# Leaving out TensorE's idle products in a two-layer mixer and expert trunk

## The reference

```python
for layer in range(DEPTH):
    h = rmsnorm(x, norm_mix[layer])
    if layer % 2 == 0:
        y = even_mixer(h, w_in_even[e], w_out_even[e], ...)   # mLSTM heads + differential attention
    else:
        y = conv_mixer(h, w_in_odd[o], conv_w[o], w_out_odd[o])
    x = x + y
    h = rmsnorm(x, norm_ffn[layer])
    x = x + hier_moe(h, ...)      # for e in 16: (silu(t @ w_gate[e]) * (t @ w_up[e])) @ w_down[e]
return rmsnorm(x, norm_final)
```

## Time and profile before

| | |
|---|---|
| median of three runs | 1122.05 us (1121.77 to 1123.04) |
| the profiled execution's own time | 1122.41 us |
| its span, first to last instruction | 1120.7 us |
| TensorE busy | 1080.9 us, 96% |
| VectorE busy | 880.2 us, 79% |
| ScalarE busy | 666.2 us, 59% |
| mean granted TensorE clock | 0.990 |

### The profile page before, as it was taken

One profiled execution on the slowest core, in us unless ns is written; L12 is line 12 of the kernel. 1 busy time (PEld: TensorE's weight loads), 2 busy tenths in 40 slices (PEclk: granted clock), 3 DMA queues, 4 the chain that ended last, 5 costly groups with the idle time before them and its releaser, 6 DMA issues.

```text
span 1120.7 us, 15231 instructions
## 1 busy us (share of the span) xinstructions
PE 1080.9 (96%) x5343; PEld 815.3 (73%) x5343; DVE 880.2 (79%) x1136; ACT 666.2 (59%) x845; POOL 109.9 (10%) x159
## 2 busy tenths in 40 slices
PE   7999999999999999999998999999999999999994
PEld 5777777678877777777776888878967777777772
DVE  5256755787889999999998452654699999999997
ACT  5224444523488888888875513222488888888872
POOL 2010000212111000000012000000120000000023
PEclk9999999999899999999999999999999999999997
DMA  9742222212389999999999322332199999999984
GB/s 323 199 142 76 85 85 76 75 57 76 113 288 395 406 393 397 408 398 409 405 372 341 125 92 76 113 101 88 76 320 394 402 400 396 409 395 406 408 309 176
DMA packets 78643, 285.89 MB, mean 255 GB/s; under 512 B 17687, under 2 KB 17687, under 8 KB 62204
## 3 DMA queue, kind: packets, MB, share of 16 engines
q1 hardware_dynamic: 66396, 241.64, 56.5%
q0 software_dynamic: 8464, 30.42, 8.3%
q10 hardware_dynamic: 3728, 13.11, 2.9%
HBM read 266.27 MB, written 20.20 MB: 256 GB/s over the span
## 4 chain that ended last, share of the span: by engine, by line
PE 86%; DVE 7%; ACT 2%; DMA 2%; issue 2%; POOL 1%; ACTq 0%; DVEq 0%; POOLq 0%; SPq 0%
PE ps L1801 26%; PE ps L1803 25%; PE ps L1802 25%; DVE w_split L1048 2%; PE ps L2135 2%; DMA arena<-h_rows_dram,arena 1%; PE ps L2071 1%; PE ps L1776 1%; ACT w_split L654 1%; PE ps L2049 1%; PE ps L1885 1%; PE ps L2159 1%; PE ps L2000 1%; DVE arena L1239 1%; DMA x_sb<-in_x 1%
## 5 line engine op out<-in xcount | busy, mean ns | idle before, releaser
L1048 DVE TENSOR_TENSOR w_split<-ring,w_split 128x1024 fp32r<-128x1024 f32 x428 | 510.9, 1220 | 43.5 <-ACT w_split L654 32.1
L654 ACT CAST w_split<-ring 128x1024 fp32r<-128x1024 f32 x428 | 445.9, 1052 | 128.0 <-PE ps L1803 125.8
L1801 PE MATMUL ps<-w_split,hT 128*96 128x512 f32 (+2 forms) x976 | 385.8, 395 | 3.5 <-DVE arena L1250 1.8
L1803 PE MATMUL ps<-w_split,hT 128*96 128x512 f32 (+2 forms) x976 | 379.1, 388 | 0.0
L1802 PE MATMUL ps<-w_split,hT 128*96 128x512 f32 (+2 forms) x976 | 378.7, 388 | 0.0
L1801 PEld LDWEIGHTS ps<-w_split,hT 128*96 128x96 f32 (+1 forms) x976 | 163.0, 167 | 64.2 <-DVE arena L1250 3.9
L1803 PEld LDWEIGHTS ps<-w_split,hT 128*96 128x96 f32 (+1 forms) x976 | 162.7, 167 | 59.9
L1802 PEld LDWEIGHTS ps<-w_split,hT 128*96 128x96 f32 (+1 forms) x976 | 163.1, 167 | 53.9
L1801 PE MATMUL ps<-hT,w_split 128*128 128x512 f32 (+1 forms) x384 | 144.8, 377 | 3.2 <-DVE hT L1084 2.5
L1802 PE MATMUL ps<-hT,w_split 128*128 128x512 f32 (+1 forms) x384 | 142.8, 372 | 0.0
L1803 PE MATMUL ps<-hT,w_split 128*128 128x512 f32 (+1 forms) x384 | 142.7, 372 | 0.0
(11 more groups left out here) (254 smaller groups left out, 900.9 us busy)
## 6 DMA issues: line engine op xcount, KB each, us to landing
ring<-in_exp_w_gate SPq DMA_DIRECT2D x64, 1024.0 KB, 11.8
ring<-in_exp_w_up SPq DMA_DIRECT2D x64, 1024.0 KB, 11.9
ring<-in_exp_w_down SPq DMA_DIRECT2D x64, 1024.0 KB, 12.4
ring<-in_w_in_even SPq DMA_DIRECT2D x14, 1024.0 KB, 13.4
y_rows_dram<-arena ACTq DMA_DIRECT2D x32, 384.0 KB, 7.0
ring<-in_w_in_odd SPq DMA_DIRECT2D x12, 1024.0 KB, 6.2
ring<-in_w_out_even SPq DMA_DIRECT2D x4, 1024.0 KB, 5.0
h_rows_dram<-arena POOLq DMA_DIRECT2D x8, 512.0 KB, 3.2
```

What stands on the lines that cost most here:

```text
L654: ins = s.copy(hi_of(c), raw(c))
L1048: ins = v.tensor_tensor(lo_of(c), raw(c), hi_of(c).bitcast(F32), ALU.subtract)
L1801: mm(out, a[0], b[0], start=start, stop=False)
L1803: return mm(out, a[0], b[1], start=False, stop=stop)
```

## The change

The helper `keep_busy` and all its calls go. Nothing takes their place: TensorE stands at the next wait, or at once runs the next instruction.

```diff
-            def keep_busy(n, bank):
-                for _ in range(n):
-                    mm(ps[:, bank, :], ones16[:, :], later[:, 0:1].broadcast_to([P, 512]), start=True, stop=True)
...
             pe.wait_ge(consts_ready, 8)
-            keep_busy(11, 7)
             turn_h(0, 0)
             turn_h(0, 1)
-            keep_busy(8, 7)
...
             last.then_inc(gate_cols_full, 1)
-            keep_busy(11, 3)
             pe.wait_ge(gate_cols_ready, 1)
...
                 last.then_inc(rank_full, 1)
-                keep_busy(2, 0)
                 gather_first(2, range(4, KD))
                 gather_first(3)
                 slot_index(l)
...
             def last_rows(l):
-                keep_busy(4, 0)
                 pe.wait_ge(y_half0, E * (l + 1))
...
             turn_h(2, 1)
             pe.wait_ge(x_freed, 1)
-            keep_busy(9, 4)
             pe.wait_ge(tr_act, tiles_copied(2, 1, True))
             pe.wait_ge(tr_dve, tiles_copied(2, 1, False))
             first_piece(0)
```

## The result

The changed kernel takes 1131.4 us in the median of five executions (1126.43 to 1131.54), against 1122.05 us; the ratio is 1.0068, 95% interval 1.0047 to 1.0089, or +7.6 us. The forecast was 1125.0 us, +2.9, in a range up to 1127.6: the direction holds, the size is less than half of the measured one, and the measured time lies above every rival's too. The profiled execution took 1131.4 us, its span is 1129.7 us, 9.0 more than before.

The account below looks back on a forecast made before the run. TensorE, busy 96% of the span and 86% of the last-ending chain, was taken as the bound. Entrance +1.8, attention +1.3, routing -1.3, last rows -0.1 and first piece +1.2 summed to +2.9 us: 1125.0 us, range 1121.8 to 1127.6.

Parts of the forecast that it names:

- every rival's: Four rivals: clock holds 1122.4 (chance 0.27), late clock 1128.2 (0.15), routing falls go 1120.1 (0.07), attention swallows delay 1123.4 (0.06).
- the first piece: Convolution mixer, 9 products removed from a wait: fall likely at three chances in four, +1.2 us (0 to 1.7).
- the length of a fall: Clock at half for 3.4 us, eight dense products at 0.20 us extra each: 1.6 us per fall.
- 1.3 at attention: Ahead of attention, 11 products removed from a wait: one fall expected, possibly beginning inside the wait, +1.3 us (0 to 1.7).
- Routing: 2 products on the chain in each layer: removing them gives back 1.3 us (0.9 to 1.3), number of falls unchanged.
- Entrance: Kernel start, 11 + 8 products removed: slower first turn plus late clock rise, +1.8 us (0.8 to 2.6).
- the turn of tile 0: Entrance: eight transposes at half clock end 0.8 us later, delaying the first real product by that much.
- the last rows: Behind the last experts, 4 products per layer fill a wait for copies: gain 0.1 us (0.1 to 0.3), no fall.
- The rival on the late clock: Transposes not counting as activity: late rise at entrance, costlier falls at attention and first piece, one more; +6.2 us, chance 0.15.

Follow-up runs that it names:

- a2: The changed kernel measured a third time, beside the kernel before: ratio 1.0072, +8.1 us.
- e2: The kernel before without only the 11 idle products ahead of attention: ratio 1.0047, +5.3 us.
- f2: The kernel before with all idle products removed but the 2 in each layer's routing: ratio 1.0057, +6.4 us.
- a1: The changed kernel measured a second time, in more executions, beside the kernel before: ratio 1.0062, +7.0 us.
- e2b: Second measurement of the kernel before without the 11 idle products ahead of attention: ratio 1.0027, +3.0 us.
- e3: The kernel before without only the 2 idle products in each layer's routing: ratio 1.0006, +0.7 us.
- e1: The kernel before without only the two entrance calls (11 and 8 idle products): ratio 1.0030, +3.4 us.
- e4: The kernel before without the 9 idle products ahead of the convolution mixer's first piece and the 4 in each last_rows: ratio 1.0018, +2.0 us.
- f1: The kernel before keeping idle products at entrance and attention only; routing, last rows and first piece without: ratio 1.0007.
- s1: The kernel before with 23 instead of 11 idle products ahead of attention: ratio 1.0017, +1.9 us.
- b2: The kernel before, unchanged, measured once more beside itself for spread and another profile: ratio 1.0006.

## Why the prediction was wrong

**What held.** TensorE's path bounds the kernel; the eleven at the entrance, the eight, the attention call and the nine stand in waits, and taking them out started nothing earlier. The clock rose late and it fell ahead of attention. That the time moved the way I forecast owes something to luck: 1.2 of the +2.9 us stood for a fall at the first piece that never came, while the losses in routing, which had no term, did.

**The step that failed: the length of a fall.** I took a fall as 3.4 us long, "That is my price for a fall with dense work behind it", 1.6 us at most and 1.3 at attention. All three falls of the trace before had that length, and I read it as a property of falls. In the six profiles in which attention's call was empty the fall lasted 6.8 us in four (the changed kernel, a2, e2, f2) and 3.4 us in two (a1, e2b). In the four it began 0.8 to 1.4 us ahead of the first scores, so that its first stretch was partly a wait, and work at half speed went on beyond it. In the two it began 0.1 us ahead of the scores or 0.8 behind them. The part from gate columns to mLSTM took 2.4 to 2.7 us more in the four and 1.5 in the two: double my price, and above my upper bound of 1.7, in most.

**Routing: the term farthest off.** I gave it -1.3 us and wrote of the falls there that they "are not brought by the change and I leave their number as it is". The number held well enough: three before, four, three and three in the changed kernel's profiles. The length didn't. In both routings together the clock was down for 10.2 us in the kernel before, in both its profiles, and for 20.5, 20.5 and 13.7 us in the changed kernel's. In the first of these profiles that made +1.2 and +2.9 us where I had -1.3 for both; beside the same profile of the kernel before, a1's two routings took 3.0 us more and a2's 0.3. Why the falls there grew stays open. The gain itself was mis-sized too: "These stand on the chain itself" was right for the earlier trace rows, but at equal time on the low clock the two products are worth 0.3 to 0.4 us in each layer, some 0.7 and not 1.3, and e3's 1.0006 shows nothing of it in the mean.

**Entrance: a term mis-sized.** +1.8 (0.8 to 2.6) against 2.5, 2.3 and 2.3 in the three profiles of the changed kernel, 3.6 in e1's. The 0.8 us for the turn of tile 0 came out as 0.75 to 0.90. I leaned to the lower half because transposes held a full clock; in four of the five profiles with an empty entrance they did not lift it. I took the rise as 3.9 us behind the first real product at most; it came 4.0, 3.4 and 3.2 us behind in the changed kernel, a2 and f2, and 6.1 in e1. In the fifth, a1, they did, and a fall in the wait behind them took the gain back, which I had named as possible and given no price.

**The first piece and the last rows.** +1.2 and -0.1. The idle stretch was as long as I said (2.61 us ahead of 614.28 in the changed kernel), yet the clock stayed at 1.00 there in all six profiles in which the call was empty. e4 alone measured +2.0 (0.8 to 3.1), f1, which contains it, +0.8 (-0.9 to +2.5). Nothing is lost at the piece itself; whether these calls lengthen the falls in layer 1's routing, as the six profiles hint, stays open.

**The rival on the late clock** (0.15, 1128.2 us) came nearest in time, and half by its own reasons: the clock was late and the fall at attention cost more, but there was no fall at the first piece, and the rule on transposes that it rested on did not hold in a1. The Trainium skill, page "TensorE: Matmul & The Clock Gate", Part 4 on PE-mode transpose, says that transposes don't count as activity; a1's clock rose at 12.84 us behind the transposes of two tiles and nothing else, so for float32 transposes of 128x128 the measurement decides against the page. In the other four profiles with an empty entrance they did not lift it.

**The range** was built from one profile and three times within 1.3 us. The executions of the kernel before spread over 5.8 to 7.7 us within the four later sets (25 to 35 in each) and those of the changed kernel over 8.9 (17 in all, 1126.43 to 1135.33). And its upper end, 1127.6, lay below a rival of its own at 1128.2. A profile shows one draw; the falls in routing are at other moments in each.

**What stays open:** 2 to 3 us of the 7 to 8 lie behind attention, mostly in the routings, as longer falls. Lying later by 2.2 or 3.5 us did not bring them in the mean (s1, e1), and routing's own products are not needed for them (f2, +6.4) and leave nothing to find alone (e3). That a fall at attention makes long falls in routing more likely fits e2, f2 and the three profiles of the changed kernel; that the empty piece and last rows do so fits all six profiles without them. Neither was shown, and no experiment took the nine out without the four.

## What to carry to other kernels

An idle product in a wait is worth what the next dense stretch would lose on a low clock: here 2.3 to 3.6 us at a cold start and 1.5 to 2.7 at a wait of 2.9 us, for products that cost nothing as long as they end within the wait (s1's surplus cost 1.9 us). Five of the eleven at attention were enough here, and in routing no worth of them could be measured. Take each call out singly, and over many executions, as one profile has its own falls; the mean clock of every execution tells more than one profile. Price a fall by where it may begin and what work stands around it, and not by the length of another fall.

## What the runs showed of the hardware

The busy time of a stretch alone did not tell what the clock did next. At the full clock a stretch busy for 1.70 of 3.41 us was not followed by a fall, and one busy for 1.81 us was, a2's ahead of attention:

```profile
90.12:93.53 3.41, 1.81 (x14) 1.00 0.16 24
93.53:96.94 3.41, 2.12 (x7) 0.50 0.98 351
```

At half, stretches busy for 2.48 (the changed kernel at 94.13), 2.57 (e2 at 91.53) and 2.73 us (e1 at 14.33) were followed by another at half, though a product takes twice as long there. In e4, which was otherwise the kernel before up to there, the clock stayed down in routing for 10.2 us in which TensorE was busy throughout, mostly with router logits and gathers:

```profile
292.07:295.48 3.41, 2.93 (x28) 1.00 0.00 0
295.48:298.89 3.41, 3.41 (x17) 0.50 0.76 304
298.89:302.30 3.41, 3.41 (x20) 0.50 0.78 311
302.31:305.72 3.41, 3.41 (x18) 0.50 0.00 0
```

Where a fall comes differs between executions of one kernel: the kernel before had it at 288.20 and 305.26 us in one profile, at 299.24 in another, b2's.
